# Stick-breaking attention worked by head pairs, with the magnitude of z formed by VectorE

## The reference

```python
def stick_breaking_attention(q, k, v):          # 8 heads of 64, blocks of 128 queries
    z = jnp.einsum('bthd,bshd->bhts', qb, k).astype(jnp.float32) * (dh ** -0.5)
    strict = (key_pos[None, :] < q_pos[:, None])[None, None]
    log_beta = jax.nn.log_sigmoid(z)
    log_one_minus = jnp.where(strict, log_beta - z, 0.0)
    suffix = lax.cumsum(log_one_minus, axis=3, reverse=True) - log_one_minus
    a = jnp.where(strict, jnp.exp(log_beta + suffix), 0.0).astype(v.dtype)
    return jnp.einsum('bhts,bshd->bthd', a, v)

# in dsa_attention: the index scores, and the 128 best keys of each query
    rel = jax.nn.relu(jnp.einsum('bthd,bsd->bths', qib, ki))
    score = jnp.einsum('bths,bth->bts', rel, wib).astype(jnp.float32) * idx_scale
    top_score, idx = lax.top_k(score, topk)
```

## Time and profile before

| what | value |
|---|---|
| median of 3 runs | 2440.68 us |
| profiled execution | 2432.89 us |
| its span | 2430.9 us |
| PE busy | 1887.3 us (78%) |
| DVE busy | 1427.8 us (59%) |
| ACT busy | 993.5 us (41%) |
| POOL busy | 639.3 us (26%) |
| mean granted TensorE clock | 0.838 |

### The profile page before, as it was taken

How to read it: one execution, slowest core, us unless ns; L and a number is a source line. 1 busy time by engine, 2 the same in 40 slices (tenths; PEclk the granted TensorE clock), 3 DMA queues, 4 the chain that set the end, 5 groups by cost and what they waited for, 6 DMA issues and landing times.

```text
span 2430.9 us, 38013 instructions
## 1 busy us (share of the span) xinstructions
PE 1887.3 (78%) x14768; PEld 1178.9 (48%) x14768; DVE 1427.8 (59%) x3252; ACT 993.5 (41%) x2400; POOL 639.3 (26%) x570
## 2 busy tenths in 40 slices
PE   5999999999766653433334698888888885999999
PEld 3877557776433310100001353345666553677887
DVE  6742774464776677777777857775344333223554
ACT  3123535623433333333333575844444212343443
POOL 0000000000444455555554433443332231000000
PEclk8999999999878655555555797688999997999999
DMA  8921002232999999999999999999999997313555
GB/s 304 330 88 70 1 9 70 64 111 70 367 420 419 420 420 417 419 416 418 417 419 406 400 418 392 415 401 419 417 418 417 417 418 303 114 53 108 185 178 170
DMA packets 123617, 712.13 MB, mean 293 GB/s; under 512 B 14592, under 2 KB 15744, under 8 KB 57648
## 3 DMA queue, kind: packets, MB, share of 16 engines
q0 software_dynamic: 74608, 542.25, 54.1%
q1 hardware_dynamic: 48592, 167.33, 19.8%
q10 hardware_dynamic: 240, 0.16, 0.0%
HBM read 707.56 MB, written 2.13 MB: 292 GB/s over the span
## 4 chain that ended last, share of the span: by engine, by line
PE 49%; DMA 31%; ACT 7%; DVE 6%; POOL 3%; issue 3%; ACTq 0%; SPq 0%; DVEq 0%
DMA arena<-experts,eidx 31%; PE psum L696 8%; PE psum L697 8%; PE psum L698 8%; PE psum L986 6%; DVE arena L1942 4%; POOL arena L1912 3%; PE psum L1277 2%; PE psum L1104 2%; PE psum L827 2%; ACT sq L1571 1%; ACT arena L1563 1%; PE psum L803 1%; PE psum L1299 1%; PE psum L1154 1%
## 5 line engine op out<-in xcount | busy, mean ns | idle before, releaser
L1942 DVE CUSTOM_DVE_ANT_0 arena<-arena 128x1024 f32<-128x1024 f32 x560 | 680.0, 1224 | 411.2 <-DMA arena<-experts,eidx 380.6
L1912 POOL DMA_INDIRECT arena<-experts,eidx x512 | 623.2, 1217 | 889.8 <-PE psum L986 717.0
L986 PE MATMUL psum<-arena,sq 32*32 32x512 f32 x8192 | 419.2, 855 | 474.0 <-ACT sq L1571 458.3
L986 PEld LDWEIGHTS psum<-arena,sq 32*32 32x32 f32 x8192 | 68.4, 121 | 717.2 <-ACT sq L1571 672.4
L1557 ACT ACTIVATE arena<-arena 128x2 f32<-128x2 f32 x256 | 52.0, 203 | 732.2 <-DVE arena L1942 731.4
L696 PE MATMUL psum<-hn_high,w_high 128*128 128x512 f32 (+1 forms) x432 | 181.3, 420 | 16.3 <-DVE hn_low L1939 15.3
L697 PE MATMUL psum<-hn_low,w_high 128*128 128x512 f32 (+1 forms) x432 | 176.0, 407 | 0.0
L698 PE MATMUL psum<-hn_high,ring_low 128*128 128x512 f32 (+1 forms) x432 | 174.6, 404 | 0.0
L1299 PE MATMUL psum<-n_t,ring 128*128 128x256 f32 x704 | 164.9, 390 | 0.6 <-DVE n_t L1939 0.6
L1299 PEld LDWEIGHTS psum<-n_t,ring 128*128 128x128 f32 x704 | 132.9, 193 | 48.9 <-issue 30.7
L1571 ACT ACTIVATE sq<-sq,arena 128x32 f32<-128x32 f32 x512 | 136.7, 313 | 24.1 <-ACT arena L1563 0.4
(11 more groups left out here) (319 smaller groups left out, 3201.6 us busy)
## 6 DMA issues: line engine op xcount, KB each, us to landing
ring<-w_stream SPq DMA_DIRECT2D x262, 512.0 KB, 4.0
arena<-w_ada SPq DMA_DIRECT2D x48, 512.0 KB, 6.7
arena<-experts,eidx POOLq DMA_INDIRECT x512, 13.1
arena<-cum_rows POOLq DMA_DIRECT2D x1, 2112.0 KB, 10.1
x<-xT SPq DMA_DIRECT2D x1, 2048.0 KB, 12.6
arena<-rel_rows POOLq DMA_DIRECT2D x1, 2048.0 KB, 15.2
arena<-sub_keys POOLq DMA_DIRECT2D x1, 1024.0 KB, 6.3
outT<-hn_rest SPq DMA_DIRECT2D x8, 128.0 KB, 8.8
```

The lines of the kernel that those rows point to most:

```text
L986: last = mm(bank(4 + 2 * odd + a)[QUART * b:QUART * b + QUART, :], diag[k, s, :], rows[k, s, D + a * 512:D + (a + 1) * 512], start=c == 0, ...
L1912: nc.gpsimd.indirect_dma_start(rows[:, s, :], None, experts, bass.IndirectOffsetOnAxis(ap=eidx[:, n // P % 2, n % P:n % P + 1], axis=0)).t ...
L1942: return V.tensor_tensor_reduce(out=out, in0=a, in1=b, scale=1.0, scalar=0.0 if op1 == ALU.add else -TAKEN, op0=op0, op1=op1, accum_out=accum)
```

## The change

The stage goes by pairs of heads. Heads 2p and 2p+1 use partitions 0 to 63 and 64 to 127 of q and k. A step is one tile of one pair, so there are 16 steps (pair p, tiles 3, 2, 1, 0). In each step TensorE makes z of the step two ahead for both heads (`z_pair`), the sums of this step, and the weighted values of the step before, two heads alternating. z of a pair lies in two neighbouring banks (0 and 1, or 2 and 3), and VectorE, ScalarE and POOL take both heads in one instruction each. The sums turn over three banks (4 to 6), the weighted values go to bank 7.

Abs on ScalarE is gone. VectorE forms -|z| from PSUM in two passes, 2 min(z, 0) and then minus z (`minus_magnitude`), and Exp takes it without a scale. The strict mask stays a product.

The top-k is no longer spread over the stage: `masks(i)` runs whole behind the scores of index block i. z of step 0 is issued halfway through the last v projection. At the end, scores 0 and the first half of gate tile 0 stand ahead of the last weighted values.

```diff
+        def z_pair(step):
+            if step >= 2:
+                pe.wait_ge(sp_done.sem, sp_done.ready(step - 2))
+            for e in range(2):
+                z_product(bank(z_bank(step) + e, T - i * P), p, e, i, True, True).then_inc(z_done.sem, 1)
...
+        def sums(step):
+            pe.wait_ge(sp_gated.sem, sp_gated.ready(step))
+            for e in range(2):
+                item = 2 * step + e
+                pe.wait_ge(a_done.sem, a_done.free(item, 3))
+                z_product(out[e], p, e, i, True, False)
+            for e in range(2):
+                mm(out[e][:, 0:P], ident[:], strict[:], start=False, stop=False)
+            for e in range(2):
                 for j in range(i, TT):
-                    last = mm(us_all[n][:, (j - i) * P:T - i * P], neg_tri[:] if j == i else neg_ones[:],
-                              sp[j], start=False, stop=j == TT - 1)
+                    last = mm(out[e][:, (j - i) * P:], neg_tri[:] if j == i else neg_ones[:],
+                              sp_of(p, j)[:, e, :], start=False, stop=j == TT - 1)
                 last.then_inc(u_done.sem, 1)
...
+        z_pair(1)
+        for step in range(HP * TT):
+            if step + 2 < HP * TT:
+                z_pair(step + 2)
+            sums(step)
+            if step:
+                weighted(step - 1)
...
         scores(0)
+        half_gate(0, 0)
+        weighted(HP * TT - 1)
... (ScalarE)
+        soft_exp(0)
+        soft_log(0)
         v_out(TT - 1)
+        soft_exp(1)
+        soft_log(1)
         high(S_GATE)
         high(S_GATE + 1)
+        for step in range(HP * TT):
+            if step + 2 < HP * TT:
+                soft_exp(step + 2)
+            weights(step, 0)
+            if step + 2 < HP * TT:
+                soft_log(step + 2)
+            weights(step, 1)
... (VectorE: masks(i) is now called inside the index loop)
+        def minus_magnitude(step):
+            a = az[TT - 1 - step % TT]
+            dve.wait_ge(z_done.sem, z_done.ready(2 * step + 1))
+            if step >= TT:
+                dve.wait_ge(yb_done.sem, yb_done.ready(2 * (step - TT) + 1))
+            z = z_both(step)
+            steps(V.tensor_scalar(a, z, 0.0, 2.0, ALU.min, ALU.mult))
+            steps.wait()
+            V.tensor_tensor(a, a, z, ALU.subtract).then_inc(abs_done.sem, 1)
...
+        minus_magnitude(0)
+        softplus(0)
+        minus_magnitude(1)
+        for step in range(HP * TT):
+            if step:
+                softplus(step)
+            if step + 2 < HP * TT:
+                minus_magnitude(step + 2)
+            if step < 2:
+                low(S_GATE + step)
+            if step > TT and step % TT == 1:
+                take_pair(step // TT - 1)
```

More of the change, by code:

```diff
@@ L816, in sums @@
[L816 to L825, removed]
+            def z_pair(step):
+                p, i = step // TT, TT - 1 - step % TT
+                if step >= 2:
+                    pe.wait_ge(sp_done.sem, sp_done.ready(step - 2))
+                for e in range(2):
+                    z_product(bank(z_bank(step) + e, T - i * P), p, e, i, True, True).then_inc(z_done.sem, 1)
@@ new lines, in sums @@
+            def sums(step):
+                p, i = step // TT, TT - 1 - step % TT
+                pe.wait_ge(sp_gated.sem, sp_gated.ready(step))
+                out = [bank(u_bank(step, e), T - i * P) for e in range(2)]
+                for e in range(2):
[5 more added lines that the diff above has]
+                for e in range(2):
@@ L826, in sums, with weighted @@
                     for j in range(i, TT):
-                        last = mm(us_all[n][:, (j - i) * P:T - i * P], neg_tri[:] if j == i else neg_ones[:],
-                                  sp[j], start=False, stop=j == TT - 1)
+                        last = mm(out[e][:, (j - i) * P:], neg_tri[:] if j == i else neg_ones[:],
+                                  sp_of(p, j)[:, e, :], start=False, stop=j == TT - 1)
                     last.then_inc(u_done.sem, 1)
[L831 to L840, removed]
+            def weighted(step):
+                p, i = step // TT, TT - 1 - step % TT
+                pe.wait_ge(a_done.sem, a_done.ready(2 * step + 1))
+                if i == TT - 1:
+                    pe.wait_ge(yb_taken.sem, yb_taken.free(p, 1))
+                for first, last in ((0, P), (P, T - i * P))[:1 + (i < TT - 1)]:
+                    for e in range(2):
+                        m = 2 * p + e
+                        ins = mm(bank(7, last - first, i * P + first)[64 * e:64 * e + 64, :],
+                                 v[:, i, (NH + m) * DH:(NH + m + 1) * DH], az[i][:, e, first:last],
+                                 start=i == TT - 1, stop=i == 0 and first > 0)
+                        if last == T - i * P:
+                            ins.then_inc(yb_done.sem, 1)
@@ L842, in _, with first_z @@
+            def first_z():
+                pe.wait_ge(dense_act.sem, dense_act.ready(A_V + 2))
+                z_pair(0)
+            v_pair(TT - 1, first_z)
             pe.wait_ge(dense_act.sem, dense_act.ready(A_V + 3))
             pe.wait_ge(relu_done.sem, relu_done.ready(23))
[L844 to L851, removed]
+            z_pair(1)
@@ L2046, in _, with masks @@
             steps.wait()
+            def masks(i):
+                w = P * (i + 1)
+                dve.wait_ge(relu_used.sem, relu_used.ready((i - 1) * NH + NH - 1))
+                steps(V.tensor_scalar(score[i], score[i], IDX_SCALE, None, ALU.mult))
+                steps.wait()
+                steps(V.tensor_tensor(score[i][:, w - P:w], score[i][:, w - P:w], causal[:], ALU.add))
+                steps.wait()
+                for r in range(TOPK // 8):
+                    steps(V.max(col[:, 0:8], score[i]))
+                    steps.wait()
+                    steps(V.match_replace(score[i], col[:, 0:8], score[i], TAKEN))
+                    steps.wait()
+                steps(V.tensor_scalar(mask[i], score[i], 0.5 * TAKEN, -GATED, ALU.is_gt, ALU.mult))
+                steps.wait()
             n = 0
@@ L2096, in take_y @@
                 tell(dve, steps, y_taken)
-            choose_keys = masks()
-            for m in range(NH):
-                softplus(m)
-                if m >= 2 and m % 2 == 0:
-                    take_pair(m // 2 - 1)
-                for _ in range(6):
-                    next(choose_keys, None)
-                if m < 2:
-                    low(S_GATE + m)
-            for _ in choose_keys:
-                pass
+            minus_magnitude(0)
+            softplus(0)
+            minus_magnitude(1)
+            for step in range(HP * TT):
+                if step:
[6 more added lines that the diff above has]
+                    take_pair(step // TT - 1)
             take_pair(HP - 1)
```

146 lines of the change are left out of this document (54 added, 92 removed).

## The result

| what | before | after |
|---|---|---|
| median of 5 runs each | 2439.73 us (2431.74 to 2443.09) | 2453.33 us (2447.76 to 2454.43) |
| profiled execution, its span | 2432.89, 2430.9 | 2451.71, 2449.8 |
| PE busy | 1887.3 us | 1880.3 us |
| DVE busy | 1427.8 us | 1451.1 us |
| ACT busy | 993.5 us | 976.6 us |

The ratio is 1.0054 with a 95% interval of 1.0039 to 1.007: slower, by 13.6 us between the medians, where 9.0 were forecast (2449.7 us). The mark moved by 15.8 us. The two profiled executions lie 18.8 us apart, more than the medians: executions of one kernel spread over 7 to 11 us here, so differences of time are read from the medians and places from the mark.

The account below looks back on a forecast made before the run. TensorE was taken to bound the stick-breaking stage, VectorE's top-k rounds lying under it. Start (+19.6), pair stage and tail summed to +4.1 us at full clock; clock +4.9 made +9.0, 2449.7 us, range 2439 to 2459.

Parts of the forecast that it names:

- The mark: TensorE's point at 357.26 us before, gate tile 0's second half done and scores of s=2 starting; forecast at 361 to 368.
- third rival: Pair stage: the clock falls once in each later pair from the 2 us waits, three at 3.2; +18.6, 2459 us, chance 0.12.
- Rounds in the blocks, start +19.6: Index blocks: all 16 rounds behind each block's scores, VectorE's rounds ending at 257.5, first sums at 261.7 instead of 242.12.
- Clock in the blocks, 3.3: Index blocks: new idle stretches lower TensorE's clock, costing about 2.2 us in block 3 and 0.6 taken for block 2.
- Prices of VectorE's passes: Pair stage: both passes over 1024 elements from PSUM take 2.45 us; 0.69 each by a two-per-cycle price.
- The chain in the second step, a wait of 2.0 and 2.4 per pair: Pairs 1 to 3: VectorE's passes, take_pair and softplus take 4.9 us against TensorE's 2.9; 0.4 more waiting in other steps.
- TensorE's work per pair, 19.86: Pair stage: TensorE's products for one pair sum to 19.86 us, against 25.5 for two heads before.
- the rival with serial products: Pair stage: z, z again and weighted products of two heads don't run beside each other; +25, 2466 us, chance 0.04.
- Clock in the later pairs, reckoned at nothing: Pair stage: the sum held no low-clock cost for pairs after the first; the first pair was given 1.2 us.
- Tail, 6.2 and 0.4 for the clock: From the last weighted product to the mark: 6.2 us instead of 11.4, plus 0.4 for a low clock.
- Abs on ScalarE, "goes and costs nothing": Pair stage: ScalarE's Abs goes and costs nothing, since ScalarE had 50 us of slack there.
- The second rival: Pair stage: VectorE doesn't hold TensorE, a pair takes 19.9 and the 12.5 us of waits go; -8.4, 2432 us, chance 0.07.

Follow-up runs that it names:

- no rounds: The changed kernel with the 48 top-k rounds left out (scaling, causal mask and compare stay, chosen keys not the reference's): 2427.55 us, ratio 0.9957.
- the fourth experiment: The changed kernel with 18 products nobody reads filling TensorE's idle time (2 in block 2, 9 in block 3, 7 behind the last v projection): 2449.7 us, ratio 1.005.
- the second experiment: The changed kernel with only VectorE's order altered, take_pair moved ahead of the passes: 2442.79 us, ratio 1.0017.

## Why the prediction was right, and where its sizes were off

The direction and the time were right, and so was the mechanism of the start. The mark was not: 373.08 lies outside the 361 to 368 given as a sign, since the pair stage and the tail were reckoned too cheap. The outcome lies between the forecast (+9.0) and its third rival (+18.6). That the time came within 4 us of the forecast is in part luck: the median moved 2.2 us less than the mark, and the first pair cost less than reckoned.

- **Rounds in the blocks, start +19.6.** Right. With the kernel before around it, the same move cost 20.0 us at the first strict mask, with the low clock in the blocks in it. In after VectorE had no gap over 1.2 us between 172 and 262 and ended its rounds at 261.6. That is the forecast's 257.5, the 1.2 us by which the trace is later before anything that the change touches (block 1 ends at 178.0, not 176.8), and 2.9 more.
- **Clock in the blocks, 3.3.** Right: those 2.9 us. Block 3 ran at 0.50 and gave a pair of 512-wide scores in 2.76 us. Without the idle time (no rounds) the clock was 1.00, and VectorE needed 8.09 and 9.15 us for blocks 2 and 3 with their low parts where after needed 9.43 and 10.81: 3.0 us went with the low clock.
- **Prices of VectorE's passes.** Right to the hundredth: 1.22 us each over 1024 elements, 0.42 over 256, so 0.69 was not their price. The Trainium skill (VectorE: DVE Perf Modes, "Why PSUM operands drop a tier") says that an fp32 operand in PSUM holds VectorE to one element per cycle; these rows agree: 768 elements more cost 0.80 us, 1.04 ns each. A TENSOR_SCALAR over 512 took 0.69 from PSUM (265.64 in after) and 0.43 from SBUF (261.14).
- **The chain in the second step, a wait of 2.0 and 2.4 per pair.** The chain was as reckoned (passes, take_pair, softplus), and its size nearly so: 0.35 + 1.70 + 0.58 = 2.63 us. What it left out is where TensorE meets it first: the single bank 7 of the weighted values, emptied by take_pair, ahead of the z banks, emptied by the softplus. Moving take_pair alone took 1.28 of the 2.63 away. So the sign "one wait near 2 us in front of a z product" came otherwise: 1.70 in front of a weighted product, and 0.58 in front of z.
- **TensorE's work per pair, 19.86.** 0.7 too much: 19.13 in the two kernels in which TensorE bounds. Half of it is the strict mask, 0.55 for two heads (294.46 to 295.01 in after) and so 2.2 per pair instead of 8 x 0.32 = 2.56; the row that I took, 284.00 to 284.32, was one product alone. The heads' products do run beside each other (z and z again of two heads, 2 x 768 columns, in 1.49 us from 292.97 to 294.46, as long as 768 columns of one head took before), so the rival with serial products is out.
- **Clock in the later pairs, reckoned at nothing.** This is the term that failed. The third rival named it: the clock falls in each later pair behind the waits. It does, in all three, at 1.56 us and not 3.2, since the clock is back by 304.0 and only that much of a pair runs slowly. The sum of a pair is 19.13 of work, 2.63 of waits, 1.56 of low clock and 0.54 that are left over: 23.86, where the sum had 19.86 and 2.4, 22.3 (the list of signs says 22.1). That the 0.54 are the emptying and refilling of TensorE around its waits is a guess; no run takes it apart. The pair of the fourth experiment in which the clock did not fall took 22.2, 1.6 less. The Trainium skill (TensorE: Matmul & The Clock Gate, "A second HAM failure mode: psum-queue depth-cycling") describes short idle times between groups that make the clock swing; with an order that waits 2.63 us per pair the trace agrees, with one that waits 1.35 the pairs stayed at 2.4 GHz. Waits of 2.63 us are not always followed by it, as that one pair shows.
- **Tail, 6.2 and 0.4 for the clock.** From the end of the last weighted values to the mark it took 8.1 us (365.0 to 373.08). VectorE's part was as reckoned (2.9), the half gate tile ran mostly at the low clock, 4.5 instead of 2.8.
- **Abs on ScalarE, "goes and costs nothing".** True of ScalarE, and the wrong question. Leaving it there is worth 22.6 us of the mark: without the two passes of VectorE the waits and the low clock of the pairs are gone, and a part of the start. Two things change at once there, a shorter chain for each z (Abs takes 1.02 us over 1024 elements, the passes 2.4) and less in VectorE's order ahead of softplus and take_pair; the second experiment shows only what take_pair's place is worth. The second rival (VectorE does not hold TensorE) would have needed exactly that.

Summed from the forecast's mark of 366.3: 1.2 by which the trace is late before the change, 0.6 more up to the first strict mask, 3.6 net in the stage (three periods 4.8 over, the rest of it 1.2 under), and 1.5 at the tail make 373.2; measured 373.08. The median moved 2.2 us less than the mark.

## What to carry to other kernels

Work that lies under the bounding engine is free only where it lies: the rounds cost nothing in the TensorE-bound stage and 20 us in front of it. VectorE had 47 us of gaps there, but the rounds are 63 us, and what doesn't fit makes TensorE wait, run on at the low clock and start late. With 35 rounds there and 13 in the stage the start was 3.7 us late and no more. Before an operation is given to an engine with slack, follow what stands behind it in that engine's order once per period and which bank or buffer it frees, a single result bank above all; 2.63 us of waits of the bounding engine here made a pair 4.7 us longer (23.86 for 19.13). And when two engines have slack, compare the two chains that release a buffer and not the busy time: with Abs on ScalarE, which then was busy 28.3 of 49 us, TensorE kept its own 19.13 us per pair.

## What the runs showed of the hardware

Filling an idle stretch with products that nothing reads kept the granted clock at 1.00 in that stretch (214 to 226 us), but block 3 behind it, TensorE busy 8.00 of 8.00 us with products of 64 rows, still had 0.64 on the mean. Whether the kind of product decides that was not tried.

Whether waits are followed by the low clock can differ within one run: with equal waits one pair took 22.2 us and the next 23.9. It also differs between kernels at the same place. Behind the wait of 2.9 us at the tail the stretch from the 256-wide scores to the mark ran wholly at the full clock in two of the changed kernel's variants (3.63 us), wholly at the low clock in one (6.41, take first), and in part at the low clock in the others (5.15 in after). What decides it stays open, and so up to 2.8 us of a tail can be of this kind and not of the edit.
